# Where a gathered row product stands among the projections of a one-core decoder step

## What is computed

```
n = rmsnorm(x);  z = n @ w_in                    # queries, keys, values, gates, conv channels
h = x + concat(rms(attention), rms(conv)) @ w_out
q = rmsnorm(h) @ wq                              # 8 heads x 2 x 128, scored against 128 + 128 keys
eidx, g = the best 16 of 128 x 128 pairs, per token and head
act = gelu(sum_d n[t, d] * u_tab[eidx[t, k], d]) # 128 experts per token
h = h + sum_k g[t, k] * act[t, k] * v_tab[eidx[t, k], :]
y = h + sigmoid(rmsnorm(h) @ w_gate) * (p @ w_ple)
```

## Time and profile before

| | |
|---|---|
| median of three runs | 2573.87 us |
| the profiled execution, its own time | 2575.46 us |
| its span in the profile | 2573.6 us |
| mean granted TensorE clock over the span | 0.776 |
| busy: TensorE matmul, VectorE, GpSimd, ScalarE | 66%, 45%, 35%, 13% |
| bytes moved by DMA | 908.75 MB, mean 353 GB/s |
| of them gathered by POOL (queue q0) | 671.13 MB |

### The profile page before, as it was taken

The page is one execution under the profiler, slowest core; times in us unless marked ns, Lnnn a source line. Parts: engine busy times, 40 slices in busy tenths (PEclk is TensorE's granted clock), DMA queues, the critical chain, the costliest instruction groups (busy, mean ns, idle before and its releaser), DMA issues.

```text
span 2573.6 us, 21559 instructions
## 1 busy us (share of the span) xinstructions
PE 1704.7 (66%) x8372; PEld 932.7 (36%) x8372; DVE 1151.2 (45%) x2141; ACT 333.6 (13%) x731; POOL 897.4 (35%) x644
## 2 busy tenths in 40 slices
PE   7999988998987659688687332233223332577677
PEld 3445665696775437433366000000000000122224
DVE  2010213134445755543533666565565765544342
ACT  1000232010002322200100100101001002001002
POOL 0000000012224334221433455665666655555330
PEclk9998996998998677598689656666665665787788
DMA  9953382779999799998998999999999999999996
GB/s 318 351 170 119 107 301 101 277 247 411 388 379 366 303 376 368 342 384 336 417 391 346 413 418 421 421 422 421 422 421 421 421 421 418 402 416 416 416 417 218
DMA packets 215844, 908.75 MB, mean 353 GB/s; under 512 B 17350, under 2 KB 40879, under 8 KB 131808
## 3 DMA queue, kind: packets, MB, share of 16 engines
q0 software_dynamic: 92160, 671.13, 63.3%
q1 hardware_dynamic: 123368, 235.41, 25.8%
q10 hardware_dynamic: 216, 0.86, 0.1%
HBM read 895.31 MB, written 14.53 MB: 354 GB/s over the span
## 4 chain that ended last, share of the span: by engine, by line
DMA 48%; PE 42%; DVE 3%; ACT 3%; issue 2%; POOL 2%; SPq 0%; DVEq 0%; ACTq 0%; PEldq 0%; POOLq 0%
DMA arena<-in_peer_v,arena 32%; PE bank L1725 8%; PE bank L2154 5%; DMA arena<-in_peer_u,arena 5%; PE bank L2169 4%; DMA arena<-in_w_in 4%; DMA arena<-in_peer_wq 3%; PE bank L1799 3%; DMA arena<-in_w_out 3%; PE bank L1936 2%; PE bank L1912 2%; PE bank L2104 2%; PE bank L2274 2%; PE bank L2084 2%; DMA arena<-in_state_win 1%
## 5 line engine op out<-in xcount | busy, mean ns | idle before, releaser
L1521 DVE CUSTOM_DVE_ANT_0 arena<-arena 128x2048 f32<-128x2048 f32 x320 | 731.0, 2292 | 643.2 <-DMA arena<-in_peer_u,arena 639.5
L2154 PE MATMUL bank<-arena 128*32 128x512 f32 x2560 | 456.2, 823 | 661.2 <-DVE arena L1530 503.7
L675 POOL DMA_INDIRECT arena<-in_peer_u,arena x320 | 545.1, 1704 | 833.0 <-DVEq L1500 580.5
L680 POOL DMA_INDIRECT arena<-in_peer_v,arena x320 | 352.0, 1100 | 763.6 <-PE bank L2154 733.3
L2154 PEld LDWEIGHTS bank<-arena 128*32 128x32 f32 x2560 | 68.9, 127 | 1001.7 <-DVE arena L1530 510.1
L1725 PE MATMUL bank<-arena 128*128 128x512 f32 (+2 forms) x544 | 216.9, 559 | 5.2 <-PE bank L1725 4.1
L2169 PE MATMUL bank<-arena 128*128 128x192 f32 x1024 | 191.9, 351 | 24.2 <-DMA arena<-in_w_in 22.6
L2169 PEld LDWEIGHTS bank<-arena 128*128 128x128 f32 x1024 | 183.4, 206 | 45.5 <-DMA arena<-in_w_in 29.8
L1725 PEld LDWEIGHTS bank<-arena 128*128 128x128 f32 (+1 forms) x544 | 101.4, 207 | 117.0 <-issue 116.6
L987 ACT ACTIVATE arena<-arena 128x4 f32<-128x4 f32 x80 | 16.9, 211 | 874.7 <-DVE arena L1521 874.5
L2274 PE MATMUL bank<-arena 128*128 128x512 f32 x256 | 119.9, 626 | 0.0
(11 more groups left out here) (267 smaller groups left out, 1533.3 us busy)
## 6 DMA issues: line engine op xcount, KB each, us to landing
arena<-in_w_in SPq DMA_DIRECT2D x22, 2048.0 KB, 9.1
arena<-in_w_in SPq DMA_DIRECT2D x32, 1024.0 KB, 15.2
arena<-in_w_out SPq DMA_DIRECT2D x8, 2048.0 KB, 9.7
arena<-in_peer_wq SPq DMA_DIRECT2D x8, 2048.0 KB, 8.3
arena<-in_w_out SPq DMA_DIRECT2D x16, 1024.0 KB, 14.6
arena<-in_peer_wq SPq DMA_DIRECT2D x16, 1024.0 KB, 23.5
arena<-in_ple_gate SPq DMA_DIRECT2D x32, 512.0 KB, 15.3
arena<-in_ple_gate SPq DMA_DIRECT2D x6, 2048.0 KB, 12.3
```

The lines of the kernel that those rows point to most:

```text
L675: pool.indirect_dma_start(u_row[j], None, I["peer_u"][0], bass.IndirectOffsetOnAxis(idx[:, i, c + j:c + j + 1], 0)).then_inc(u_in[j], 16)
L680: pool.indirect_dma_start(v_row[j], None, I["peer_v"][0], bass.IndirectOffsetOnAxis(idx[:, i, c + j:c + j + 1], 0)).then_inc(v_in[j], 16)
L1521: dve.tensor_tensor_reduce(out=u_row[j], in0=u_row[j], in1=rep_of(i), scale=1.0, scalar=0.0, op0=ALU.mult, op1=ALU.add, accum_out=a4[:, pa ...
L2154: ins = pe.matmul(bank[i % 2][32 * q:32 * q + 32, :], diag[:, k % 2, j, :], v_row[j][:, 512 * q:512 * q + 512], start=(s == 0 and j == 0), ...
```

## The change

On TensorE, in steps 17 to 20 and 23 to 26 one weighted tile stands behind each quarter of the block, where before all four stood behind the block. In steps 8, 9 and 10 the first of the three items stands ahead of the weighted tiles and the other two behind them. In step 16 the weighted tiles come first and all three items behind them. On ScalarE, step 16's items all stand behind the gelu. The waits for the diagonals and for the accumulator move into the first weighted tile of a step. VectorE, POOL and SP are untouched; no instruction that computes or moves data is added or removed.

```diff
@@ scalar
             items = items_of(k) if k < EARLY else ()
-            if items:
+            if items and k != 16:
                 before_gelu(items[0])
...
-            for v in items[1:]:
+            for v in items[0 if k == 16 else 1:]:
                 before_gelu(v)
             behind_gelu(k)
@@ tensor, project_b
             for q in range(4):
                 f = 4 * blk + q
+                if q:
+                    weighted_tile(17 + blk, q - 1)
                 pe.wait_ge(rb_in[ring_of(f)], ring_count(f))
...
                 ins.then_inc(rb_used, 1)
+            weighted_tile(17 + blk, 3)
@@ tensor, queries_b
             for q in range(4):
                 f = 16 + 4 * blk + q
+                if q:
+                    weighted_tile(23 + blk, q - 1)
                 pe.wait_ge(rb_in[ring_of(f)], ring_count(f))
...
                 ins.then_inc(rb_used, 1)
+            weighted_tile(23 + blk, 3)
@@ tensor, weighted_rows and weighted_tile
         def weighted_rows(k):
-            i, s = divmod(k, SSTEP)
-            if s == 0 and i >= 2:
-                pe.wait_ge(acc_ev, i - 1)
-            pe.wait_ge(diag_ready, k + 1)
             for j in range(4):
                 weighted_tile(k, j)
         def weighted_tile(k, j):
             i, s = divmod(k, SSTEP)
+            if j == 0:
+                if s == 0 and i >= 2:
+                    pe.wait_ge(acc_ev, i - 1)
+                pe.wait_ge(diag_ready, k + 1)
             pe.wait_ge(v_in[j], 16 * (k + 1))
@@ tensor, the loop over steps
                 for j in range(4):
                     late_quarter(k + 1, j)
-                    if j == 0:
-                        pe.wait_ge(diag_ready, k + 1)
                     weighted_tile(k, j)
                 continue
...
-            for v in items_of(k):
+            items = items_of(k)
+            if 17 <= k < 21 or 23 <= k < 27:
+                item(k)
+                continue
+            for v in items[0:0 if k == 16 else 1]:
                 item(v)
             weighted_rows(k)
+            for v in items[0 if k == 16 else 1:]:
+                item(v)
```

## The result

The changed kernel takes 2554.6 us (median of 14 runs, 2538.15 to 2570.07), the kernel before 2575.19 (14 runs, 2568.91 to 2583.67): a ratio of 0.9922, interval 0.9902 to 0.9942. It is 20.6 us faster, where 43.5 were forecast. Its runs spread over 32 us and those of the kernel before over 15, but 33 later runs of the kernel before spread over 28. The profiled execution of the changed kernel took 2548.46 us, 27.0 less than that of before.

A forecast was written before the change was run, and what follows sets the result against it. Transfers were taken as the bound behind the 24th slice, at 419 GB/s, with holes of 69.8 us ahead. Terms 15 + 12 + 9 + 7.5 = 43.5 us off 2575.46 gave 2532.0, as a median 2531 us; range 2508 to 2556.

The forecast's parts named there:

- sum rule: All bytes must move in either kernel, so a hole filled early is time saved at the end if the stream stays full.
- The cuts: Weighted tiles between quarters, steps 17 to 20 and 23 to 26: 0.09 us for each of 24 tiles, about 2 us, covered.
- rival 4: Slower: weighted tiles wait for v tiles, then quarters run at 1.2 GHz; 2579 us, or 2621 with two waits; chance 0.05.
- my sign of wrong: In the two projection stages, a granted clock below the 0.90 and 0.92 of the kernel before.
- Steps 17 to 20 and 23 to 26, 15 + 12 us: The projection blocks: tiles behind each quarter free v buffers earlier, winning 15 of 18.4 us and 12 of 15.7 us.
- 12.6 MB and 30.0 us: Projection steps: gathers of 8.39 MB plus four quarters of 1.05 MB a step, and the time these transfers take.
- Steps 8 to 10, 7.5 us: Weighted tiles ahead of two items: one set of v tiles won, 10 us, less 2.5 for the chain; net 7.5 us.
- the longer chain: Steps 9 to 11: the TensorE, VectorE and ScalarE chain grows by 2.5 us; diagonals still 28 to 31 us apart.
- costed at nothing: Steps 11 to 15, 21 and 22 keep their order, and a shift ahead of them goes through.
- rival 1: Chains hold in steps 8 to 10 and 16, transfers idle later in steps 11 to 15; 2549 us, chance 0.18.
- Step 16, 9 us: Gelu and weighted tiles run ahead of the sample values; step 17's v gathers leave earlier, winning 9 of 11.2 us.
- The rate of 405: Sign of right: transfers at 405 GB/s or more throughout, from 1090 us to the end of step 26.

## Why the prediction was right and wrong

- **The mechanism** (holes ahead of a stream that is full behind them, made by v gathers that wait for weighted tiles) was right, and so was the sum rule: every execution ends earlier by its lead at 1440, within 2.8 us.
- **The cuts** cost next to nothing, as forecast (0.08 us each), and rival 4 (waits for v tiles, then the slow clock) did not come. From 1090 to 1230 one weighted tile waits for its v tile, 1.2 us, and the granted clock is 0.89 (0.90 before). The 0.82 of 1330 to 1420 looks like my sign of wrong, but cut where the last block ends it is two stages:

```profile
1385.00:1420.00 35.00, 17.11 (x188) 7.58 (x184) 18.92 (x48) 5.00 (x7) 16.86 (x15) 0.67 1.02 393
1330.00:1385.00 55.00, 43.93 (x302) 36.31 (x302) 17.02 (x18) 2.77 (x11) 14.94 (x14) 0.91 0.87 341
```

  At 0.91 the blocks run as before; they only end sooner, and what follows has little work for TensorE.
- **Steps 17 to 20 and 23 to 26, 15 + 12 us: the step that failed.** "The v gathers fill the time in which the stream ran dry" was priced as nearly all of both holes, 27 of 34.1 us. Measured are 7.7 + 4.6 = 12.3 by the ratios of the parts and 5.9 + 2.0 = 7.9 by the leads. That leaves 15 to 19 of the 23 us that are missing.
  - In steps 23 to 26 the 12.6 MB and 30.0 us were taken for all four blocks. The last fetches no weights for a successor, so its 20.0 us of gathers stand against 25.6 us of TensorE. Its hole was 9.2 us and is 9.7; half of its products bring it to 3.3.
  - In steps 17 to 20 the rate rose from 364 to 389, 8.4 us of the 18.4. The steps are 30 to 32 us apart, as forecast. The prediction's low end had the late u gathers leave a hole in each step; two dents are there, and what makes them is open.
- **Steps 8 to 10, 7.5 us: not clearly wrong in size** (4.8 by the leads, 8.5 by the ratio, with a wide interval), but the account was. The 10 us were won, and the longer chain did not come (26.4 us between diagonals, not the 28 to 31 I gave). Instead, steps 11 to 15, "costed at nothing", did not pass the shift on: about half went back there, since TensorE's waits of some 20 us for the sample's loads let its tiles move by 7.5 us only. That is rival 1's idle stretch, and "steps 11 to 15 longer by what was won ahead of them" stood among the signs of wrong. Without these waits the whole 10 us stay.
- **Step 16, 9 us: right or somewhat high**, 6 to 8 with the cuts behind it, and 3.9 alone.
- **Rival 1's 2549 us** is the nearest number by luck: it has 27 us for the projections, which brought less than half of that, and nothing for steps 8 to 10 and 16. The far end of the range, 2556, took 12 as the low end of steps 23 to 26, where the text has 3; with that it would be 2565.

The ratios of the parts, with steps 16 to 20 as one, add up to 8.5 + 15.7 + 4.6 = 28.8 us, the leads to 18.5; the whole is 20.6 to 26.6 by the medians and 27.0 in the profiled execution. The rate of 405 from 1090 on that I asked for was missed (389).

## What to carry to other kernels

A hole that is filled early counts only up to the next place where the engine that frees the buffers is held by something else, here loads that share the DMA with the moved stream. So walk the stream from the edit to where it stays full, and list each load there that an engine waits for, with the size of its pieces. Count the bytes of a stage block by block: the last one fetches nothing for a successor and may have another bound. And price an edit in the company that it will have, as step 16 is worth 6 to 8 us with the cuts and at most half of that alone. Last, read a lead against several executions of both programs: single ones differed by 4 to 6 us in a stretch.

## What I had not expected of the hardware

Beside a full stream of gathers with 8 KB rows, a load of 512 KB in pieces of 1 KB took 17.7 to 32.3 us to land, and one was there for TensorE only 34 us after its issue; two issued while the stream had holes took 3.9 and 5.5. 1 MB in rows of 8 KB took 9.1 to 14.4. The four pairs' loads as they are cost 17 to 18 us of the kernel's time, nearly as much as the whole change brought. A second queue for part of them helped in the kernel before (0.9974, 0.9952 to 0.9996); in the changed one 0.9878 stands against 0.9922, with intervals that touch.
